# A hybrid decoder step: decode attention on four groups of 32 partitions, with the probabilities turned by VectorE's block transpose

## The reference

```python
for _, d in ATT_PATTERNS:                 # (128, 1), (512, 4), (2048, 16)
    idx = w_buf + jnp.arange(t)[:, None] - steps[None, :] * d
    s = jnp.einsum('bthd,btkhd->bthk', q, kg) * (HEAD_DIM ** -0.5)
    lse = jax.nn.logsumexp(s, axis=-1)
    p = jnp.exp(s - lse[..., None])
    outs.append(jnp.einsum('bthk,btkhd->bthd', p, vg))
```

## Time and profile before

| | |
|---|---|
| time of the launch, median of 3 runs | 1509.22 us (1509.13 to 1509.26) |
| the profiled execution, its own time | 1509.26 us |
| its span, from first to last instruction | 1507.3 us |
| TensorE busy | 1494.9 us (99%) |
| VectorE busy | 824.6 us (55%) |
| ScalarE busy | 584.6 us (39%) |
| granted TensorE clock | 0.998 of full speed |

### The profile page before, as it was taken

One profiled execution on the slowest core, in us unless ns is written; L12 is line 12 of the kernel. 1 busy time (PEld: TensorE's weight loads), 2 busy tenths in 40 slices (PEclk: granted clock), 3 DMA queues, 4 the chain that ended last, 5 costly groups with the idle time before them and its releaser, 6 DMA issues.

```text
span 1507.3 us, 27167 instructions
## 1 busy us (share of the span) xinstructions
PE 1494.9 (99%) x11095; PEld 1414.1 (94%) x11095; DVE 824.6 (55%) x1075; ACT 584.6 (39%) x792; POOL 221.7 (15%) x316
## 2 busy tenths in 40 slices
PE   9999999999999999999999999999999999999997
PEld 9999777777778999999999999999999999999997
DVE  7669899964566677444444444444444433333434
ACT  6333434446545354333333333333333323333332
POOL 7874344500630000000000000000000000000100
PEclk9999999999999999999999999999999999999999
DMA  7557899999987444444444444444444444444442
GB/s 270 187 160 246 293 370 371 335 367 356 345 316 263 155 149 145 154 153 144 150 153 147 146 153 150 144 151 153 145 148 153 147 147 153 152 143 153 150 151 105
DMA packets 83282, 296.59 MB, mean 197 GB/s; under 512 B 9984, under 2 KB 11136, under 8 KB 82816
## 3 DMA queue, kind: packets, MB, share of 16 engines
q1 hardware_dynamic: 82624, 294.34, 57.6%
q10 hardware_dynamic: 576, 1.08, 0.2%
HBM read 289.31 MB, written 5.43 MB: 196 GB/s over the span
## 4 chain that ended last, share of the span: by engine, by line
PE 90%; DVE 5%; POOL 2%; issue 1%; ACT 1%; DMA 0%; DVEq 0%; ACTq 0%
PE ps L2001 20%; PE ps L2002 20%; PE ps L2000 20%; PE ps L1846 6%; PE ps L1884 3%; PE ps L1848 3%; PE ps L1890 2%; PE ps L1885 2%; PE ps L1658 2%; PE ps L1687 2%; DVE wlo L986 1%; PE ps L1952 1%; PE ps L1953 1%; PE ps L1951 1%; POOL par L1425 1%
## 5 line engine op out<-in xcount | busy, mean ns | idle before, releaser
L1300 DVE TENSOR_TENSOR wlo<-raw,whi 128x1024 fp32r<-128x1024 f32 x264 | 325.2, 1232 | 519.9 <-ACT whi L863 519.8
L863 ACT ACTIVATE whi<-raw 128x1024 fp32r<-128x1024 f32 x264 | 279.9, 1060 | 606.2 <-PE ps L2002 601.7
L2002 PE MATMUL ps<-xh,wlo 128*128 128x320 f32 x1400 | 432.6, 309 | 0.0
L2000 PE MATMUL ps<-xh,whi 128*128 128x320 f32 x1400 | 432.6, 309 | 0.0
L2001 PE MATMUL ps<-xl,whi 128*128 128x320 f32 x1400 | 432.6, 309 | 0.0
L2000 PEld LDWEIGHTS ps<-xh,whi 128*128 128x128 f32 x1400 | 262.8, 188 | 0.0
L2002 PEld LDWEIGHTS ps<-xh,wlo 128*128 128x128 f32 x1400 | 262.8, 188 | 0.0
L2001 PEld LDWEIGHTS ps<-xl,whi 128*128 128x128 f32 x1400 | 262.8, 188 | 0.0
L2000 PE MATMUL ps<-hh,whi 128*128 128x320 f32 x696 | 215.1, 309 | 0.0
L2001 PE MATMUL ps<-hl,whi 128*128 128x320 f32 x696 | 215.1, 309 | 0.0
L2002 PE MATMUL ps<-hh,wlo 128*128 128x320 f32 x696 | 215.1, 309 | 0.0
(11 more groups left out here) (335 smaller groups left out, 1804.1 us busy)
## 6 DMA issues: line engine op xcount, KB each, us to landing
raw<-in_w_gu SPq DMA_DIRECT2D x176, 512.0 KB, 3.5
raw<-in_w_dn SPq DMA_DIRECT2D x88, 512.0 KB, 3.5
raw<-in_w_in SPq DMA_DIRECT2D x78, 512.0 KB, 5.9
kv<-in_ck SPq DMA_DIRECT2D x76, 512.0 KB, 6.7
kv<-in_cv SPq DMA_DIRECT2D x64, 512.0 KB, 7.7
raw<-in_w_out SPq DMA_DIRECT2D x32, 512.0 KB, 3.7
raw<-in_cv SPq DMA_DIRECT2D x16, 512.0 KB, 7.7
out_kv<-z SPq DMA_DIRECT2D x2, 1280.0 KB, 12.4
```

The costliest lines, as they stand in the source:

```text
L863: act.activation(whi[:, j % SPL, :], raw[:, j % RAW, :], ACT.Copy).then_inc(S["w_hi"], 1)
L1300: v.tensor_tensor(wlo[:, j % SPL, :], raw[:, j % RAW, :], whi[:, j % SPL, :].bitcast(F32), ALU.subtract) \
L2000: t_.matmul(out, whi[:, slot, w], ah[:, k, :], start=(k == 0), stop=False)
L2002: last = t_.matmul(out, wlo[:, slot, w], ah[:, k, :], start=False, stop=(k == 2 * units - 1))
```

## The change

The groups of 32 partitions stand for keys now, not for heads. Group j has keys 32j to 32j+31 of each tile of 128, for all heads; the heads' four groups g lie one behind the other in the free dimension. `sall` becomes 128 x 4 x 352: for each g, 320 old keys and 32 columns for new ones.

- **Scores**: 4 steps (one for each g) over all 1280 keys in place of 5 over 256. Each step has K in two pieces of 768 and 512 KB (`K_PARTS`), and 16 matmuls of 192 or 128 columns. A K step is released as a whole. The new keys' scores (4 batches' worth, 32 columns) go to one group only, that of batches 0 to 3 or 4 to 7; the other groups' columns are set to a large negative number by `no_new`.
- **Maximum**: it now lies in four partition groups. ScalarE copies it together (`spread_maxima`), VectorE reduces (`maxima`), ScalarE copies it back with its scale (`spread_bias`), and four exponentials follow, one for each g (`exponent`). All of this is in slot +4.
- **Turning**: TensorE's transposes and ScalarE's copies go. VectorE turns all 1408 columns in blocks of 32 x 32 (`turn_probabilities`, slot +5), which puts keys on partitions.
- **Sums**: four matmuls with one column add the partial sums over the groups (`sum_probabilities`, bank 6, slot +5). VectorE takes the reciprocal behind the turn (`inverse_sums`).
- **Values**: as before but in slots +6 to +10; new values in the same tile shape as old ones, over all 128 rows, of which the upper 64 are zero. Output in slot +11. Batches begin one slot later (37, 43, ..., 79), so that outputs are in the same slots as before.
- **Ring**: K and V share 7 x 4 KB of each partition by size, and V can use the eighth place.

```diff
-START_OF = (36, 42, 48, 54, 60, 66, 72, 78)
-TURN, VALUES, OUTPUT = 5, 7, 12
+START_OF = (37, 43, 49, 55, 61, 67, 73, 79)
+TURN, VALUES, OUTPUT = 5, 6, 11
...
-                    "pt": lambda: ("pt_moved", 4 * key[1] + (key[2] + 1 if key[2] < 2 else 4)),
-                    "score": lambda: ("s_masked", 6 * key[1] + (key[2] + 1 if key[2] < 4 else 6)),
+                    "score": lambda: ("s_masked", KS * key[1] + key[2] + 1) if key[2] < KS - 1 else ("new_masked", key[1] + 1),
+                    "norm": lambda: ("s_sum", key[1] + 1),
...
+            def spread_maxima(b):
+                act.wait_ge(S["s_max"], b + 1)
+                for j in range(4):
+                    act.activation(quads[0:32, j, :], smax[32 * j:32 * j + 32, 0:4], ACT.Copy).then_inc(S["s_spread"], 1)
+            def spread_bias(b):
+                act.wait_ge(S["s_top"], b + 1)
+                for j in range(4):
+                    act.activation(sbias[32 * j:32 * j + 32, 0:4], sbias[0:32, 4:8], ACT.Copy, scale=-SCALE).then_inc(S["s_bias"], 1)
             def exponent(b):
-                act.wait_ge(S["s_max"], b + 1)
-                act.activation(sall[:], sall[:], ACT.Exp, bias=smax[:, 7:8], scale=SCALE, accum_out=rsum[:, 0, b:b + 1]).then_inc(S["p_exp"], 1)
+                act.wait_ge(S["s_bias"], 4 * b + 4)
+                for g in range(4):
+                    act.activation(sall[:, g, :], sall[:, g, :], ACT.Exp, bias=sbias[:, g:g + 1], scale=SCALE,
+                                   accum_out=psums[:, b, g:g + 1]).then_inc(S["p_exp"], 1)
...
+            def maxima(b):
+                dve.wait_ge(S["s_spread"], 4 * b + 4)
+                v.tensor_reduce(sbias[0:32, 4:8], quads[0:32].rearrange("p j g -> p g j"), AX.X, ALU.max).then_inc(S["s_top"], 1)
+            def turn_probabilities(b):
+                dve.wait_ge(S["p_exp"], 4 * b + 4)
+                if b:
+                    dve.wait_ge(S["v_used"], KEY_TILES * b)
+                if b < LATE:
...
+                    step(v.transpose(ptk_late[b][:], sall[:, :, KQ:KW]), wait=False)
+                v.transpose(ptk[:].rearrange("p a n -> p (a n)"), sall[:].rearrange("p a n -> p (a n)")).then_inc(S["p_turned"], 1)
+                dve.wait_ge(S["p_turned"], b + 1)
+                if b < DEC_BATCH - 1:
+                    no_new((slice(32, 64), slice(64, P)) if b + 1 < 4 else (slice(0, 32), slice(64, P)))
+            def inverse_sums(b):
+                dve.wait_ge(S["p_sums"], b + 1)
+                v.reciprocal(rsum[:, b:b + 1], ps[:, 6, 0:1]).then_inc(S["s_sum"], 1)
...
+                if i == KS - 1:
+                    pe.wait_ge(S["z_done"], 20)
+                    q = slice(32 * (b // 4), 32 * (b // 4) + 32)
+                    for f in range(NF):
+                        at = KQ + 32 * (f // 2)
+                        t_.matmul(ps[q, 6, at:at + 32], qst[:, b % 2, f, :], z[:, ZK + f, SEQ + 32 * (b // 4):SEQ + 32 * (b // 4) + 32],
+                                  start=(f % 2 == 0), stop=(f % 2 == 1), tile_position=(0, 32 * (b // 4)))
...
+            def sum_probabilities(b):
+                fill(6, "norm", b)
+                pe.wait_ge(S["fold_ready"], 1)
+                pe.wait_ge(S["p_exp"], 4 * b + 4)
+                for g in range(4):
+                    last = t_.matmul(ps[32 * g:32 * g + 32, 6, 0:1], fold[:], psums[:, b, g:g + 1], start=True, stop=True,
+                                     tile_position=(0, 32 * g))
+                last.then_inc(S["p_sums"], 1)
```

## The result

The changed kernel took 1550.04 us (median of 4 runs, 1547.88 to 1556.4) against 1509.18 for the kernel before on the same chip: ratio 1.0278, 95% interval 1.0247 to 1.031. It is slower by 2.8%, where I had forecast 0.6%, and lies outside the range. The profiled execution took 1547.88 us.

What follows compares the result with a forecast made beforehand. TensorE was taken to set the time, with VectorE and the transfers close behind. 1509.3 - 8.7 saved + 7.7 + 10.1 of two new waits = 1518.4 us, 0.6% slower; own range 1512 to 1527, with rival A 1500 to 1527.

Steps and rivals of the forecast that it cites:

- the work of the unit hides them: K tiles in pieces of 768 and 512 KB, same bytes: transfers taken as hidden behind TensorE's projection unit, no cost.
- 8.7 us saved: TensorE's net saving: 0.89 us a batch times 8, plus 0.27 six times; between 0 and 10 us.
- Term (a): TensorE in slot +4: eight transposes fall away, saving 0.85 us a batch.
- (d, e): TensorE's scores and new keys: regrouped scores put at nothing, new keys in one column group 0.4 us more a batch.
- (c): New values weighed in their neighbours' tile shape, from batch 2 on: 0.27 us saved, six times.
- The first new wait: TensorE's sums in slot +5 wait for ScalarE's exponentials: 7.7 us over all batches.
- U: Time mark of the forecast: the start of the last matmul of a projection unit.
- The second new wait: Bank 6, needed by the next scores, waits for VectorE's reciprocal behind the block transpose: 10.1 us over all batches.
- rival C: VectorE's block transpose takes 3.3 us instead of 1.65, giving 1531 us; chance 0.07.
- Rival B: Transfers become the bound, the 4 MB ring falling short: up to 1 us a batch, 1523 us; chance 0.08.
- within batch 2's waits: VectorE gets about 2 us more a batch; its 10.6 us idle is used up, counted in batch 2's waits.
- Rival A: Exponentials and reciprocal arrive in time, so the chain hides and only the saving is left: 1500.6 us; chance 0.22.

Runs made afterwards that it cites:

- run 3: Changed kernel with VectorE taking the reciprocal of the sums ahead of the block transpose instead of behind it: 1549.13 us, 1.0266.
- run 7: Kernel before, with only its exponentials moved from the end of slot +4 to slot +5, behind the weight copy: 1527.32 us, 1.0123.
- run 8: Kernel before, with four TensorE waits put in for 1, 2, 4 and 4 GpSimd operations: 1523.98 us, 1.0096.
- run 4: Changed kernel with the keys' and values' transfers, and TensorE's waits for them, left out from the third batch on: 1542.01 us, 1.0218.
- run 9: Changed kernel with maxima chain and exponentials at slot +3, block transpose at +4 (first batch's at +5), sums behind the values: 1534.25 us, 1.0172.
- run 11: Run 9 with the keys' and values' transfers, and TensorE's waits for them, left out from the third batch on: 1526.67 us, 1.0118.
- run 14: Run 12 with the large block transpose cut to a quarter (352 of 1408 columns) from the second batch on: 1531.95 us, 1.0155.
- run 15: Changed kernel with the large block transpose cut to a quarter from the second batch on: 1545.37 us, 1.0241.
- run 12: Changed kernel: maxima chain and exponentials at slot +3, all transposes at +4, reciprocal ahead of the low part, queries a slot earlier: 1537.19 us, 1.0181.
- run 17: Run 9 without the exchange of maxima, the transpose a quarter from the second batch, no key and value transfers from the third: 1514.06 us, 1.0029.
- run 1: Changed kernel with the sums behind the last value tile, in bank 4, and the reciprocal moved to slot +10: 1550.73 us, 1.029.
- run 5: Changed kernel with the maxima chain and exponentials one slot earlier, at slot +3: 1546.58 us, 1.0249.
- run 6: Run 5 with the block transpose at slot +4 instead of +5 from the second batch on: 1539.4 us, 1.0198.
- run 10: Run 9 with the values at slots +7 to +11 and the turned output at +12: 1563.23 us, 1.0357.
- run 13: Run 12 with batches starting where the kernel before has them, values seven and output twelve slots behind: 1558.6 us, 1.0334.

## Why the prediction was wrong

The direction was right, and so were the two waits that it named, and most single durations. The failed step is the one that summed the waits: it had two kinds of them, 17.8 us together, each at its own length, and put down at nothing the clock behind them, the transfers ("the work of the unit hides them") and every wait that a late VectorE or ScalarE causes at other lines. Measured on TensorE, in us, forecast and found:

| | forecast | found |
|---|---|---|
| saved | 8.7 | 14.3 |
| wait at the sums | 7.7 | 19.3 |
| wait for the reciprocal | 10.1 | 5.6 |
| waits for transfers | 0 | 6.6 |
| waits at the scan's, the prompt's and other lines | 0 | 9.5 |
| clock beside the waits | 0 | 11.8 |
| in all, slower by | 9.1 | 38.5 |

Seven of the 29 us that the sum was short by are in the two waits that it had; 28 are in the three terms at nothing; the larger saving takes 6 off.

- **"8.7 us saved": too small, some 13 to 14.** Term (a) held: slots 41 and 47 got shorter by 0.87 and 0.83 us, 0.85 forecast. I had charged scores and new keys (d, e) +0.4 a batch. Measured, the slot without scores (36) is shorter by 1.19, three slots longer by 0.22 each and the last by 0.49: together 0.04 less. A step of scores that is dropped takes its entry with it, and the new keys were near the lower bound (16 records in 0.47 to 0.50). That is 3.5 us over eight batches. (c) was not read apart.
- **"The first new wait", 7.7 us: about 19.** By batch, forecast and measured: 2.3 and 4.5, 0.9 and 1.0, 2.5 and 4.7, 1.0 and 2.2, 0.3 and 2.1 for batches 4 to 6 (all in 6), 0.7 and 4.8. In batches 1 and 3 the last to come was bank 6's copy behind the exponentials (216.05 and 304.35), in batch 6 the prompt's maximum (448.34), 0.3 us behind the exponentials. For batch 0 the exponentials end 8.1 us behind U (170.33), not 6.1. The eight small copies took 0.87 and 0.89 instead of 0.65 and 0.65; VectorE was still at the scan when the low half was due, 0.7; and the table's load, 1.28, which the trace of before also had in that slot, at 165.01, and which I had not read. Batches 5, 6 and 7 have the load too, of which the kernel before had it in 6 alone. The Trainium skill (page "ScalarE: Activation LUTs", section "What ACT_TABLE_LOAD costs") gives 1283 ns for a load and as much again, 1380, for a drain. The load agrees; a drain does not show: the copy in front ends at 174.74, and the exponential behind begins at 176.05.
- **"The second new wait", 10.1 us: 5.6.** By batch, forecast and measured: 1.0 and 0, 1.0 and 0.9, 2.0 and 1.3, 0.7 and 0, 1.9 and 2.1, 0.5 and 0, 3.0 and 1.3. For batch 0 the reciprocal ends at 183.55 and the scores start at 183.97: while TensorE waited and then ran at the low clock, VectorE caught up. I had added two waits in a loop that shares its slack. The transpose itself was right, 1.63 us against 1.65, so rival C is out; run 3 shows that without these waits the time is the same.
- **The clock: 0 in the sum, some 12 us measured.** It is missing from the working altogether. I had priced a TensorE wait at "its full length"; runs 7 and 8 show 14.6 us of waits costing 18, and gaps of 11.7 costing 14.7.
- **"The work of the unit hides" the transfers: no.** Runs 4 and 9 with 11 put them at 8 us each time. Rival B was right that they cost something and named 4.6 us; its mechanism, the room in the ring, was not tested by itself. It stood beside the forecast, not instead of it.
- **VectorE's load** I counted "within batch 2's waits". Runs 14 and 15 show 5 us for 7.7 us of its time, and in run 12 it is the engine without a gap from batch 1's transpose to batch 2's reciprocal.
- **Rival A** asked that both waits fall under 1.1 us a batch. Even with everything suspected left out (run 17) it did not come about.

The common fault: I followed one wait at a time. In slots 43 to 65 VectorE had 10.6 us idle, ScalarE stood behind TensorE, and TensorE behind both. Any delay in one is handed round: take its first visible wait away, and the next user in line waits (runs 1, 3, 5, 6, 12). What stays open is how the 39 us divide. Left out one by one, the parts give 13 (exchange of maxima), 8 (transfers), 5 (a shorter transpose) and 16 (queue places), and these overlap; the last 15.8 us of waits in run 17 were read by line but not taken apart.

## What to carry to other kernels

Where three engines hand work round with less than a microsecond of slack a slot, price a change by the whole loop: the length of the added chain, each foreign operation that stands ahead of it in each queue, and the clock behind each TensorE wait of some microseconds. When a loop's start or number of steps is shifted, look for every constant that meant "the last step" (here the slot 4 of the exponentials: a slot too late costs 18 us in the kernel before, though in the changed one putting it right gave 3, which its interval doesn't tell from nothing). When a step is moved, look for what waits for it in another engine's queue (the transpose of runs 10 and 13). And a wait that vanishes without a gain only names the next one in line.

## What the runs showed of the hardware

- The granted clock does not follow from a wait's length alone. Gaps of 2.23, 3.58 and 4.61 us in a kernel otherwise busy (run 8) cost 1.7 us of full speed each, and one of 1.30 none. In run 7 two gaps of 2.70 us differ: the clock was 1.00 from 370 to 390 us, about the one that ended at 375.3, and 0.91 from 420 to 440, about the one that ended at 427.6. And in the changed kernel, from 340 to 440 us, gaps of 2.3 to 3.1 us left it at 1.00, and the one of 4.89 from 253 us on was followed by 12 us at 0.61.
- The block transpose of 32-bit data costs 304, 532 and 1629 ns for 128, 352 and 1408 columns of 128 partitions: close to 1.04 ns a column and a fixed 0.17 us.
- A small ScalarE copy (32x4) takes 199 to 204 ns in the mean, and four in a row 0.87 to 0.89, so one per 0.21 to 0.23 us: they do not overlap.
- 8 matmuls (16 records) of 32 columns in one group of 32 columns take 0.47 to 0.50 us, where 16 records of 64 columns in four groups took 0.25.
